# Attention stage: the value products of a unit in the same round as its turns, one round behind the scores instead of two

## What is computed

```python
s = jnp.einsum('bkgqd,bksd->bkgqs', qblk.astype(jnp.float32), kf) * scale
p = jax.nn.softmax(s, axis=-1)
return jnp.einsum('bkgqs,bksd->bkgqd', p, vf)
```

## Time and profile before

| | us |
|---|---|
| median of 3 runs | 2818.67 |
| lowest and highest | 2815.82, 2820.88 |
| the profiled execution: its time | 2819.79 |
| its span | 2818.0 |
| attention stage, first scores to last output product | 367.84 to 675.95 |
| PE busy | 2277.8 (81% of the span) |
| DVE busy | 948.9 (34%) |
| ACT busy | 659.0 (23%) |
| mean granted clock of PE | 0.905 |

### The profile page before, as it was taken

The page is one execution under the profiler, slowest core; times in us unless marked ns, Lnnn a source line. Parts: engine busy times, 40 slices in busy tenths (PEclk is TensorE's granted clock), DMA queues, the critical chain, the costliest instruction groups (busy, mean ns, idle before and its releaser), DMA issues. The chain is left out here.

```text
span 2818.0 us, 38122 instructions
## 1 busy us (share of the span) xinstructions
PE 2277.8 (81%) x15898; PEld 1350.7 (48%) x15898; DVE 948.9 (34%) x1879; ACT 659.0 (23%) x1284; POOL 216.3 (8%) x299
## 2 busy tenths in 40 slices
PE   4969679998999477778797999999976188888850
PEld 0344446665555376777654555553435044443420
DVE  0045556663775353545461101102125000000117
ACT  1032066663442222322220000001021011111211
POOL 1000000000000222222100000000000300000001
PEclk9979789999999698889898999999975599999985
DMA  9540020000100123223202100102111688888855
GB/s 228 211 107 0 0 52 2 1 2 38 30 19 0 33 43 55 45 48 54 52 0 82 45 23 23 45 0 82 37 46 52 119 294 302 304 308 304 311 197 171
DMA packets 320155, 265.52 MB, mean 94 GB/s; under 512 B 168048, under 2 KB 278768, under 8 KB 319728
## 3 DMA queue, kind: packets, MB, share of 16 engines
q1 hardware_dynamic: 305552, 213.72, 26.9%
q0 software_dynamic: 9392, 31.02, 3.3%
q10 hardware_dynamic: 5040, 18.35, 1.6%
HBM read 220.87 MB, written 42.00 MB: 93 GB/s over the span
## 5 line engine op out<-in xcount | busy, mean ns | idle before, releaser
L661 PE MATMUL ps<-R 128*128 128x512 f32 (+1 forms) x816 | 299.6, 528 | 18.7 <-issue 9.3
L910 PE MATMUL ps<-R 128*128 128x512 f32 (+1 forms) x768 | 286.0, 526 | 19.2 <-DMA R<-in_w_dn_br_dram 17.1
L802 PE MATMUL ps<-R 64*64 64x64 f32 x5120 | 192.4, 238 | 100.7 <-DVE R L1511 56.2
L983 PE MATMUL ps<-R 128*128 128x512 f32 x560 | 251.1, 602 | 13.4 <-DMA R<-in_w_down_e_dram 9.5
L802 PEld LDWEIGHTS ps<-R 64*64 64x64 f32 x5120 | 182.7, 153 | 118.2 <-DVE R L1511 58.3
L661 PEld LDWEIGHTS ps<-R 128*128 128x128 f32 x816 | 157.5, 194 | 158.6 <-issue 141.2
L910 PEld LDWEIGHTS ps<-R 128*128 128x128 f32 x768 | 147.1, 192 | 151.7 <-issue 144.3
L983 PEld LDWEIGHTS ps<-R 128*128 128x128 f32 x560 | 104.4, 191 | 159.6 <-issue 158.5
L1731 DVE TENSOR_TENSOR R<-ps,R 128x256 f32<-128x256 f32 x35 | 14.9, 425 | 465.1 <-ACT R L1250 465.1
L1586 DVE TENSOR_TENSOR R<-ps,R 128x512 f32<-128x512 f32 (+1 forms) x48 | 28.9, 603 | 393.5 <-ACT R L1208 392.6
L1390 DVE TENSOR_SCALAR_CACHE_REDUCE R<-ps 128x512 f32<-128x512 f32 (+1 forms) x208 | 128.3, 666 | 65.9 <-PE ps L727 65.7
(11 more groups left out here) (236 smaller groups left out, 2727.6 us busy)
## 6 DMA issues: line engine op xcount, KB each, us to landing
R<-in_w_gate_e_dram SPq DMA_DIRECT2D x35, 1024.0 KB
R<-in_w_up_e_dram SPq DMA_DIRECT2D x35, 1024.0 KB
R<-in_w_down_e_dram SPq DMA_DIRECT2D x35, 1024.0 KB
R<-in_w_mod_dram SPq DMA_DIRECT2D x12, 2048.0 KB, 8.3
slot_output<-R ACTq DMA_DIRECT2D x35, 512.0 KB, 7.8
R<-in_w_in_dram SPq DMA_DIRECT2D x30, 512.0 KB, 5.5
R<-tu_scratch SPq DMA_DIRECT2D x160, 64.0 KB, 2.4
R<-in_x_sample_dram SPq DMA_DIRECT2D x16, 512.0 KB, 3.5
```

Source lines behind the costliest of these rows:

```text
L661: last = mm(ps[:, u % 4, 0:w], w_sb[n % NW][:, k, :], hT[:, k, c0:c0 + w], start=(k == 0), stop=(k == KD - 1))
L802: last = mm(ps[lo, bank, a * C:(a + 1) * C], lhs(a)[lo], rhs(a)[lo], start=start and (alone or a == 0), stop=stop and (alone or a == PAIRS ...
L910: mm(ps[:, o + x, 0:w], wk[:, x, k, :], hT[:, k, c0:c0 + w], start=(k == 0), stop=(k == KD - 1))
L983: last = mm(ps[:, 2, :], hsT[t % 2][:, k, :], b[:, k * 512:(k + 1) * 512], start=(k == 0), stop=(k == KD - 1))
```

## The change

The products of unit i - 1 are taken in round i, behind the turns of the same unit, and the loops of PE and ACT have one round less. The spread of a tile and DVE's output product move one round forward with them, and so does the place of the spread in the ring of banks. ACT copies the result of unit i - 1 at the place where it copied that of unit i - 2.

```diff
--- before.py
+++ after.py
@@ -276,13 +276,13 @@
         SLICE0 = list(itertools.accumulate([len(slices(i)) for i in range(NQ)], initial=0))
 
         TURNS, TURN0, FINAL = [], {}, {}
-        for i in range(NQ + 2):
+        for i in range(NQ + 1):
             if 1 <= i <= NQ:
                 for g in range(2):
                     TURN0[i - 1, g] = len(TURNS)
                     TURNS += ["dve" if j == 2 else "act" for j, _ in slices(i - 1)]
-            if i >= 2 and i % 4 == 1:
-                FINAL[(i - 2) // 4] = len(TURNS)
+            if i >= 1 and i % 4 == 0:
+                FINAL[(i - 1) // 4] = len(TURNS)
                 TURNS.append("out")
         TURN0[NQ, 0] = len(TURNS)
 
@@ -779,10 +779,10 @@
                     scores(i, slices(i)[2:])
                 if 1 <= i <= NQ:
                     turn(i - 1, 1)
-                if i >= 2:
-                    values(i - 2)
-                    if i % 4 == 1:
-                        spread((i - 2) // 4)
+                if i >= 1:
+                    values(i - 1)
+                    if i % 4 == 0:
+                        spread((i - 1) // 4)
             pe.wait_ge(S["ot_used"], NT)
 
             pe.sem_inc(S["arrivals"], 1)
@@ -1110,9 +1110,9 @@
                     if i % 4 == 0 and qt - 1 > 0:
                         act.wait_ge(S["sum_ready"], qt - 1)
                     probs(i, 0)
-                if i >= 2:
-                    qt, h4 = QH[i - 2]
-                    act.wait_ge(S["pv_mm"], i - 1)
+                if i >= 1:
+                    qt, h4 = QH[i - 1]
+                    act.wait_ge(S["pv_mm"], i)
                     if qt - 1 > 0:
                         act.wait_ge(S["ot_used"], qt - 1)
                     f(ou[qt % 2][:, h4, :], ps[:, 7, h4 * P:(h4 + 1) * P], ACT.Copy).then_inc(S["o_out"], 1)
@@ -1413,15 +1413,15 @@
                 dve.wait_ge(S["o_out"], 4 * (qt + 1))
                 v.tensor_tensor(oT[:, :, qt * P:(qt + 1) * P], ou[qt % 2], ps[:, 4 + t % 3, :].rearrange("p (a c) -> p a c", a=4), ALU.mult).then_inc(S["ot_used"], 1)
 
-            for i in range(NQ + 3):
+            for i in range(NQ + 2):
                 if i >= 4 and i % 4 == 0:
                     qt = i // 4 - 1
                     dve.wait_ge(S["p_ready"], 8 * (qt + 1))
                     if qt > 0:
                         dve.wait_ge(S["diag_ready"], 2 * qt)
                     v.reciprocal(inv_sum, sums[qt % 2]).then_inc(S["sum_ready"], 1)
-                if i >= 3 and i % 4 == 2:
-                    rows_out((i - 3) // 4)
+                if i >= 2 and i % 4 == 1:
+                    rows_out((i - 2) // 4)
                 if i < NQ:
                     score_slices(i, slices(i)[0:2])
                 if 1 <= i <= NQ:
```

## The result

| | before | after |
|---|---|---|
| median of 4 runs, us | 2819.43 | 2862.79 |
| lowest and highest | 2815.82, 2820.88 | 2860.48, 2867.21 |
| the profiled execution | 2819.79 | 2862.48 |
| attention stage, first scores to last output product | 308.1 | 347.8 |
| everything else in the span | 2509.9 | 2512.9 |

The change makes the kernel slower by a factor of 1.0158 (95% interval 1.014 to 1.0175), 43 us. The forecast was 2854.6, with 2846 to 2866 as its range.

What follows compares the result with a forecast made beforehand. PE's own work was taken to set the pace in the attention stage's latent units, so its stalls add directly: 30.3 + 3.2 + 1.5 + 3.3 - 2.4 = +35.9 us on the median 2818.67, giving 2854.6 us, range 2846 to 2866.

Steps and rivals of the forecast that it cites:

- Items 1 and 2: PE's wait for DVE's last copy before the products: 0.90 us in latent rounds, 1.37 in seven beginning with the reciprocal.
- Item 3: Rounds 10 to 39: the stall delays all behind it, ACT and DVE add nothing; 30.3 us longer together.
- Item 7: End of the stage: the last round has one set of products instead of two; -2.4 us.
- step 1: Latent rounds' wait before the products, 0.90 us by DVE's copy; wrong if named after ACT's copy or well off 0.9.
- Item 6: Rounds 8 and 9: waits of 0.59 and 0.90, products moved +2.18, less 0.37 of idle; +3.3 us.
- Item 5: Context rounds: +3.2 us in rounds 3 to 7, bound by a ring through ACT; +1.5 us in rounds 1 and 2.
- I take the clock as unchanged: PE's granted clock: assumed as in the kernel before, despite stalls leaving PE idle up to 1.4 us a round.
- The ring through ACT: Context rounds 3 to 7: turns, ACT's copies, products and exponential in a cycle, 2.47 us a round; 4.37 with spread.
- The third rival: PE's clock falls in the stalls: 2872 us if in seven reciprocal rounds, 2929 if in 31 latent rounds; chance 4%.
- Item 4: Spread one round forward: POOL's two products (2.04 us) cost nothing in latent rounds; PE waits for POOL in round 4.

Runs made afterwards that it cites:

- the two waits: Changed kernel, waiting for ACT's copies ahead of the first product, for DVE's copy only ahead of slice 2; 2836.01 us, 1.0066.
- the turned order of waits: Changed kernel with two products without use ahead of the wait in each context unit's `values`, DVE's wait the last of three; 2857.75 us, 1.0145.
- 34 products ahead: 34 products without use (result overwritten) on PE ahead of the attention stage; changed kernel 2865.52 us (1.0177), kernel before 2828.36 us (1.0054).
- the second comparison: Changed kernel run again without edit; 2859.12 us beside 2818.64 for the kernel before, 1.0155.
- the kernel with the wait alone: Kernel before, products still two rounds behind, but with the changed kernel's wait for copies they don't read; 2854.78 us, 1.0127.
- runs with products without use: PE given products whose result is overwritten: 34 or 16 ahead of the stage (both kernels), or two or five per context unit (changed kernel); 2819.74 to 2865.52 us.
- both runs that did it: Changed kernel with two or five products without use ahead of the wait in each context unit's `values`; 2857.75 us (1.0145) and 2863.99 us (1.0159).
- the waits split: Changed kernel, products waiting for each slice's copy just before reading it (2827.42 us, 1.003), or for DVE's copy only ahead of slice 2 (2836.01 us, 1.0066).
- 16 products ahead: 16 products without use on PE ahead of the attention stage; changed kernel 2862.24 us (1.0148), kernel before 2819.74 us (1.0003).

## Why the prediction was right, and where it was off

The reading of the bound held. PE was full in the latent rounds, and every idle put there came out in the time: 4.07 us more in four rounds.

*Items 1 and 2* (0.90 and 1.37 us, set by DVE's last copy) are right to the hundredth: rounds of 9.57 for 8.67, the four rounds of a tile 4.07 longer. That the price is the wait, not the new place of the products, is shown from both sides: taken out of the changed kernel it gives the 8.67 back, put into the kernel before it costs the same 39.67 for four rounds. That the copy is DVE's is shown by the two waits. *Item 3* (30.3 us): measured 30.3. Neither ACT nor DVE held up a turn. *Item 7* (-2.4): 6.25 became 3.84. One sign that the prediction gave for being wrong in step 1 did show up, ACT's copy named before L760 in most latent rounds; the two waits and the turned order of waits show that it was the name that was wrong, and not the step.

*Item 6* (+3.3): rounds 8 and 9 take 15.75 us for 12.34, so +3.4.

*Item 5* (+3.2 and +1.5 for rounds 0 to 7) is the step that was off: measured +6.1 (17.09 for 11.02) and +2.3 (9.47 for 7.15). What failed is "I take the clock as unchanged". The ring through ACT was sized rightly: at the upper level a round is 2.43 against 2.47, the one with the spread 4.46 against 4.37, and with the idle filled the rounds 3 to 7 take 14.2 against 14.25. But the forecast took the clock from the kernel before, where it had risen 7 us into the stage. Each context round of the changed kernel has PE idle before its products, and with that the clock stayed at the lower level for another 13 us; with that idle filled it rose after 7. The third rival asked the right question at the wrong place: it looked at the latent rounds, where the clock stood at 1.00 throughout, with 10% idle and stalls up to 1.37 us. Here the Trainium skill (TensorE: Matmul & The Clock Gate, A second HAM failure mode: psum-queue depth-cycling), which had been weighed and put aside, was half right: short idles between groups of matmuls go with a lower clock, worth 3.6 us in this case, yet in the two traces of the changed kernel not by a swing. There they kept a low clock low; from 400 to 680 us they did not lower a high one. Only with 34 products ahead did the clock of that kernel fall inside the stage, once, and rise again. *Item 4* is right in latent rounds. In round 4 the wait for POOL was absent in the changed kernel, since PE at the lower level was late itself, and was there (0.95) once PE ran at the upper one.

The sum: 30.3 + 3.4 + 6.1 + 2.3 - 2.4 = 39.7 us in the stage, against 35.9 forecast and 39.7 measured. The medians differ by 43.4 and, in the second comparison, by 40.5; the 3.7 us above the stage's share in the first are within what the rest of the kernel varies by.

What stays open: why the clock of the kernel with the wait alone rose 10 us into the stage, with the same 0.47 of idle in its context rounds, and not after 20. It has no products in its first round, so PE worked on end from 371.16 to 374.54, 3.4 us; but the changed kernel has stretches nearly as long in each context round (374.12 to 377.44), so this alone doesn't tell the two apart. Nor do the runs with products without use separate the idle that these close from the work that they add, and each of those runs has one trace. Shown is that filling the short idles brought the clock up early, in both runs that did it; a rule for the clock is not shown.

## What to carry to other kernels

A consumer that ran two steps behind cost nothing here on the engine that sets the pace, and one step behind it met the last copy of what it read. Look up, in the trace, when that copy ends against when the consumer would start, and the difference is the price of each round. If it must stand that close, wait for each piece where it is read; here this gave back all of it in the latent rounds. And moving work to an earlier round on an engine that is full saved nothing here: what the end gained, the start paid.

## What the runs showed of the hardware

- PE's granted clock, at the lower level when the stage begins, rose 7 us later in the kernel before (both traces), and 20 us later in the two traces of the changed kernel and in those with the waits split and with 16 products ahead, where PE stood idle for 0.47 to 0.57 us of each round of 3.8 or 3.9 (and for 0.89 more in the first). With the wait alone, with 0.47 of idle too, it rose after 10. Two products without use a round brought it back to 7 us and took 3.6 us off the context part.
- A PE that was busy at the upper level for 14 us and then idle for 2.08 was at the lower level again in the first 4 us of the stage in the changed kernel (2.98 us busy, mean clock 0.52), and some 3 us into it in the kernel before. With 29.5 us of work right up to the first scores the clock stayed up in the kernel before (1.00 from 384 to 388, busy 2.73 of 4) and fell for some 3 us in the changed kernel (0.68, busy 3.48 of 4): the busier stretch had the lower clock.
- With three waits in a row, PE's idle is put down to one engine in the profile and may be another's: ACT's L1102 was named for 0.83 us that DVE's L1408 set; with the order of the waits turned, DVE was named.
- PE starts 0.10 us after the end of DVE's copy in the changed kernel (547.09 to 547.19), and 0.05 after ACT's where that is the last (582.91 to 582.96).
- The attention stage repeats to 0.1 us (before) and 0.2 us (after) between traces, while the rest of the kernel before differs by 10 us between its two traces. A small change in such a stage is read from the stage.
